# Latent attention with values stationary, probabilities divided before the transposes, ScalarE evicting the keys, and another order of its stage

## The reference

```python
def mla(h, pos, w_down, q_norm, kv_norm, w_uq, w_ukv, w_out):
    cq, ckv, kr = jnp.split(h @ w_down, [256, 512], axis=-1)
    q = (rms_norm(cq, q_norm) @ w_uq).reshape(bsz, seq, 16, 64 + 32)
    q_nope, q_rope = q[..., :64], rope(q[..., 64:], pos)
    kv = (rms_norm(ckv, kv_norm) @ w_ukv).reshape(bsz, seq, 16, 64 + 64)
    k_nope, v = kv[..., :64], kv[..., 64:]
    k_rope = rope(kr, pos)
    # in blocks of 128 queries
    s = (einsum('bqhd,bkhd->bhqk', qn_i, k_nope) + einsum('bqhr,bkr->bhqk', qr_i, k_rope)) * 96 ** -0.5
    p = jax.nn.softmax(s, axis=-1)
    o = einsum('bhqk,bkhd->bqhd', p, v)
    return o.reshape(bsz, seq, 16 * 64) @ w_out

x = layer_norm(ALPHA * x + (1 + gate) * mla(x * (1 + scale) + shift), g, b)
```

## Time and profile before

| What | Value |
|---|---|
| Median of 3 runs | 1023.76 us (1023.01 to 1024.12) |
| Profiled execution, whole | 1025.26 us |
| Its span in the profile | 1023.2 us |
| PE, DVE, ACT busy in the span | 98%, 79%, 49% |
| Scores of unit 0 to the transposes `next` | 749.7 us to 824.3 us |

### The profile page before, as it was taken

The page is one execution under the profiler, slowest core; times in us unless marked ns, Lnnn a source line. Parts: engine busy times, 40 slices in busy tenths (PEclk is TensorE's granted clock), DMA queues, the critical chain, the costliest instruction groups (busy, mean ns, idle before and its releaser), DMA issues.

```text
span 1023.2 us, 13210 instructions
## 1 busy us (share of the span) xinstructions
PE 998.2 (98%) x5024; PEld 830.2 (81%) x5024; DVE 806.8 (79%) x1203; ACT 502.9 (49%) x756; POOL 51.4 (5%) x101
## 2 busy tenths in 40 slices
PE   7899999999999999999999999999999999999996
PEld 5678888889978778888887888888888888888885
DVE  5889898689889887888779878877878886666455
ACT  3654345376767544343546343443677654443430
POOL 1000000013311000000000000000100000000000
PEclk9999999999999999999999999999999999999999
DMA  9999999558343699989848997974332559767431
GB/s 353 400 350 407 385 380 319 184 176 293 112 147 120 208 358 364 300 289 355 280 142 320 361 317 278 374 263 143 93 98 91 171 188 325 238 201 244 167 124 42
DMA packets 72545, 254.80 MB, mean 249 GB/s; under 512 B 8801, under 2 KB 10337, under 8 KB 72482
## 3 DMA queue, kind: packets, MB, share of 16 engines
q1 hardware_dynamic: 68946, 242.91, 66.5%
q0 software_dynamic: 3104, 10.39, 3.4%
q10 hardware_dynamic: 432, 0.66, 0.2%
HBM read 252.85 MB, written 1.07 MB: 248 GB/s over the span
## 4 chain that ended last, share of the span: by engine, by line
PE 88%; DMA 4%; DVE 4%; ACT 2%; issue 1%; SPq 0%; DVEq 0%; ACTq 0%
PE bank L1921 27%; PE bank L1925 26%; PE bank L1924 26%; DMA w_raw<-in_w_dram 3%; PE bank L2332 2%; DMA arena<-in_ada_w_dram 1%; PE bank L2043 1%; PE bank L2066 1%; PE bank L2033 1%; PE bank L2054 1%; PE bank L2154 1%; PE bank L2184 0%; ACT arena L929 0%; PE bank L1894 0%; DVE w_lo L1243 0%
## 5 line engine op out<-in xcount | busy, mean ns | idle before, releaser
L1243 DVE TENSOR_TENSOR w_lo<-w_raw,w_hi 128x2048 fp32r<-128x2048 f32 (+3 forms) x162 | 345.0, 2148 | 22.8 <-ACT w_hi L895 22.7
L1921 PE MATMUL bank<-w_hi,hT_hi 128*128 128x512 f32 (+3 forms) x880 | 350.8, 399 | 9.5 <-DVE hT_lo L1780 6.4
L1925 PE MATMUL bank<-w_lo,hT_hi 128*128 128x512 f32 (+3 forms) x880 | 338.7, 385 | 0.0
L1924 PE MATMUL bank<-w_hi,hT_lo 128*128 128x512 f32 (+3 forms) x880 | 338.2, 384 | 0.0
L895 ACT ACTIVATE w_hi<-w_raw 128x2048 fp32r<-128x2048 f32 (+3 forms) x152 | 281.1, 1852 | 37.5 <-DMA w_raw<-in_w_dram 27.5
L1921 PEld LDWEIGHTS bank<-w_hi,hT_hi 128*128 128x128 f32 x880 | 165.8, 188 | 45.0 <-DVE hT_lo L1780 8.0
L1925 PEld LDWEIGHTS bank<-w_lo,hT_hi 128*128 128x128 f32 x880 | 165.7, 188 | 33.4
L1924 PEld LDWEIGHTS bank<-w_hi,hT_lo 128*128 128x128 f32 x880 | 166.2, 189 | 28.6
L1017 ACT ACTIVATE arena<-bank 128x256 f32<-128x256 f32 x88 | 33.6, 382 | 277.7 <-PE bank L1925 277.6
L1262 DVE SCALAR_TENSOR_TENSOR arena<-arena,c_row 128x1024 f32<-128x1024 f32 x131 | 155.8, 1218 | 8.2 <-ACT c_row L970 7.2
L1921 PE MATMUL bank<-w_hi,fT_hi 128*128 128x512 f32 x352 | 138.3, 393 | 1.7 <-DVE fT_lo L1801 1.7
(11 more groups left out here) (243 smaller groups left out, 867.3 us busy)
## 6 DMA issues: line engine op xcount, KB each, us to landing
w_raw<-in_w_dram SPq DMA_DIRECT2D x306, 512.0 KB, 5.8
arena<-in_ada_w_dram SPq DMA_DIRECT2D x132, 512.0 KB, 7.5
m_o<-in_ada_w_dram SPq DMA_DIRECT2D x10, 512.0 KB, 7.1
gate_row<-gate_scratch POOLq DMA_DIRECT2D x6, 512.0 KB, 5.2
arena<-in_ln_g_dram POOLq DMA_DIRECT2D x6, 512.0 KB, 4.6
arena<-in_ln_b_dram POOLq DMA_DIRECT2D x6, 512.0 KB, 6.5
w_raw<-in_w_dram SPq DMA_DIRECT2D x8, 256.0 KB, 2.8
w_raw<-in_w_dram SPq DMA_DIRECT2D x8, 192.0 KB, 2.8
```

The costliest lines, as they stand in the source:

```text
L1243: op = nc.vector.tensor_tensor(w_lo[:, j0 % RING, c], raw_of(j0)[:, c], w_hi[:, j0 % RING, c].bitcast(F32), ALU.subtract)
L1921: mm = nc.tensor.matmul(dst, a_hi, b_hi, start=start, stop=False)
L1924: nc.tensor.matmul(dst, a_lo, b_hi, start=False, stop=False)
L1925: return nc.tensor.matmul(dst, a_hi, b_lo, start=False, stop=stop)
```

## The change

It touches the latent attention alone.

1. V: values are stationary and transposed probabilities move. The outputs of the two heads, 64 rows each, go to partitions 0 to 63 and 64 to 127 of bank 5, already transposed. `owin` and its 16 transposes are gone.
2. The division moves ahead: a new VectorE step D takes the reciprocal and multiplies `mP` (128x256 for each head) before P; P waits for it (`p_ready`) where it waited for the exponentials.
3. ScalarE copies the transposed probabilities to `mpT` and the transposed keys out of bank 7 (both VectorE's before); VectorE still evicts the queries.
4. ScalarE writes the high part of V's output into `hT_hi`, VectorE the low part in a step of its own (`values_lo`), and V of the next unit waits for that.
5. The exponential's table is loaded by a small instruction behind `uq` (0, 1).
6. The latents move to blocks 4 to 7 of `hT`, the first tile's output to banks 0 and 1.
7. The order is new: the projections start with step 10 where they started with step 12, and nearly all stand between units. The low parts of the weights move with them. The residual and the normalization of tile 0 (`end`) come before V of unit 15, and the second half of slot 16 and a scaling of x come behind it.

```diff
-            before = {1: (("rq", (1, 1)),), 3: (("qkT", (1, 0)),), 4: (("uq", (2, 0)), ("rq", (2, 0))),
-                      12: (("out", (0, 0, 0)),), 13: (("out", (0, 0, 1)),), 14: (("out", (1, 0, 0)),), 15: (("out", (1, 0, 1)),),
-                      16: (("out", (2, 0, 0)),)}
+            yield from (("S", 0), ("S", 1), ("ukv", (1, 1)), ("qkT", (1, 0)), ("P", 0), ("S", 2), ("P", 1), ("V", 0), ("S", 3),
+                        ("hi", (8, 0, 1)), ("qkT", (1, 1)), ("P", 2), ("V", 1))
+            before = {4: (("uq", (2, 0)),), 5: (("uq", (2, 1)),), 6: (("ukv", (2, 0)),),
+                      7: (("qkT", (2, 0)), ("ukv", (2, 1))), 8: (("uq", (3, 0)), ("uq", (3, 1))),
+                      9: (("ukv", (3, 0)), ("ukv", (3, 1))), 10: (("out", (0, 0, 0)), ("qkT", (3, 1)), ("out", (0, 0, 1))),
+                      11: (("out", (0, 1)),), 12: (("out", (1, 0)),), 13: (("out", (2, 0)),), 14: (("out", (1, 1)),),
+                      15: (("out", (3, 0)),), 16: (("out", (2, 1)),)}
-            yield from (("out", (3, 0)), ("split", (16, 0, 1)), ("owin", (1, 1)), ("end", 0), ("out", (0, 1)), ("out", (1, 1)),
-                        ("out", (2, 1)), ("next", 0), ("out", (3, 1)))
+            yield from (("next", 0), ("out", (3, 1)))
...
+            inner = {4: (("rq", (2, 0)),), 5: (("rq", (2, 1)),), 6: (("lo", (10, 0, 1)),), 8: (("rq", (3, 1)),),
+                     9: (("qkT", (3, 0)),), 10: (("qkT", (3, 1)),), 11: (("lo", (12, 1)),), 12: (("lo", (13, 0)),),
+                     13: (("lo", (14, 0)),), 14: (("lo", (15, 0)),)}
+            outer = {5: (("lo", (9, 0, 1)),), 6: (("qkT", (2, 0)),), 7: (("qkT", (2, 1)), ("rq", (3, 0))),
+                     8: (("lo", (11, 0)),), 9: (("lo", (11, 1)), ("scale", (0, 0))), 10: (("lo", (12, 0)), ("scale", (0, 1))),
+                     11: (("scale", (1, 0)),), 12: (("lo", (13, 1)),), 13: (("lo", (14, 1)),), 14: (("lo", (15, 1)),)}
+            for n in range(4, 16):
+                yield "S", n
                 yield from inner.get(n, ())
+                yield "D", n
+                yield "V", n - 2
                 yield from outer.get(n, ())
-            yield from (("split", (16, 0, 1)), ("owin", (1, 1)), ("end", 0))
+            yield from (("end", 0), ("V", 15), ("lo", (16, 1)), ("scale", (1, 1)))
...
+        M_UNITS = {(0, 0): 2, (0, 1): 4, (1, 0): 6, (1, 1): 8, (2, 0): 10, (3, 0): 12, (2, 1): 14, (3, 1): 16}
+        M_KEYS = {0: (2, 1), 2: (2, 2), 4: (4, 3), 6: (4, 4), 8: (6, 5), 10: (8, 7), 12: (8, 6), 14: (8, 8)}
...
+                        elif stage == "exp":
+                            nc.scalar.activation(early_silu[:, :], neg_half[:, :], ACT.Exp)
+                        elif stage == "qkT":
+                            nc.scalar.activation(mkT[g % 2][:, :, t * P:(t + 1) * P],
+                                                 banks[7][0:96, :].rearrange("p (h n) -> p h n", h=4), ACT.Copy)\
+                                .then_inc(mk_ready, 1)
+                        elif stage == "P":
+                            nc.scalar.activation(mpT[:, m % 2, :], banks[4][:, :], ACT.Copy).then_inc(pT_ready, 1)
                         elif stage == "V":
+                            nc.scalar.activation(hT_hi[:, k, tok], banks[5][:, 0:P], ACT.Copy).then_inc(o_hi, 1)
...
                     elif stage == "end":
                         residual(s)
-                        norm(s, 0)
+                        values_lo(14)
+                        norm(s, 0, lambda: split_lo(base[s] + 16, (0,)))
+                    elif stage == "D":
+                        b = m % 2
                         dve.wait_ge(s_exp, A0 + m + 1)
+                        step(nc.vector.reciprocal(rden[:, m % 4, :], den[:, m % 4, :]))
+                        step.wait()
+                        for a in range(2):
+                            op = nc.vector.tensor_scalar(mP[:, b, a, :], mP[:, b, a, :], rden[:, m % 4, a:a + 1], None, ALU.mult)
+                        op.then_inc(p_ready, 1)
+            def values_lo(m):
+                dve.wait_ge(o_hi, O0 + m + 1)
+                nc.vector.tensor_tensor(hT_lo[:, k, tok], banks[5][:, 0:P], hT_hi[:, k, tok].bitcast(F32),
+                                        ALU.subtract).then_inc(o_ready, 1)
...
                     elif stage == "P":
-                        pe.wait_ge(s_exp, A0 + m + 1)
+                        pe.wait_ge(p_ready, m + 1)
...
-                            pe.wait_ge(o_att, A0 + m)
-                        for a in range(2):
-                                mm = nc.tensor.matmul(banks[5][:, a * 64:a * 64 + 64], mpT[:, m % 2, c:c + P],
-                                                      v_nat[g][:, kt, h * 64:h * 64 + 64],
-                                                      start=kt == 0, stop=kt == 1)
+                            pe.wait_ge(o_ready, O0 + m)
+                        for kt in range(NT):
+                            for a in range(2):
+                                mm = nc.tensor.matmul(banks[5][a * 64:a * 64 + 64, 0:P], v_nat[g][:, kt, h * 64:h * 64 + 64],
+                                                      mpT[:, m % 2, c:c + P], start=kt == 0, stop=kt == 1,
+                                                      skip_group_check=True)
```

More of the change, by code:

```diff
@@ L273, in build @@
         qk4_tr = sem("qk4_tr")
-        qk4_ready = sem("qk4_ready")
+        mk_ready = sem("mk_ready")
+        mq_ready = sem("mq_ready")
         c_ready = sem("c_ready")
@@ L457, in mla_plan @@
                     yield stage, m
-                    if (n, stage) == (1, "E"):
-                        yield "ukv", (1, 1)
-                    if n == 9 and stage in ("S", "V"):
-                        yield "qkT", (3, int(stage == "V"))
+                    if (n, stage) == (9, "S"):
+                        yield "qkT", (3, 0)
                 yield from behind.get(n, ())
-            yield from (("out", (3, 0)), ("split", (16, 0, 1)), ("owin", (1, 1)), ("end", 0), ("out", (0, 1)), ("out", (1, 1)),
-                        ("out", (2, 1)), ("next", 0), ("out", (3, 1)))
+            yield from (("next", 0), ("out", (3, 1)))
         def mla_vector_plan():
@@ L558, in out_banks @@
         def out_banks(s, t):
-            return ([banks[0], banks[5]], [banks[6], banks[7]])[t] if subs[s][0] == "hyb" else Y[t]
+            if subs[s][0] == "ffn":
+                return Y[t]
+            return ([banks[0], banks[5 if subs[s][0] == "hyb" else 1]], [banks[6], banks[7]])[t]
         def entry_banks(s):
@@ L1404, in residual @@
                 dve.wait_ge(h_ready, 4 * (2 * s + 2))
+                area = scratch2 if subs[s][0] == "mla" else scratch
                 for half in range(2):
                     c = slice(half * 512, half * 512 + 512)
-                    step(nc.vector.tensor_tensor(scratch[:, c], out_banks(s, 0)[half][:, :], gate_row[:, c], ALU.mult))
+                    step(nc.vector.tensor_tensor(area[:, c], out_banks(s, 0)[half][:, :], gate_row[:, c], ALU.mult))
                 for half in range(2):
@@ L1699, in mla @@
                             k, tok = 2 * v + n, slice(t * P, (t + 1) * P)
-                            op = nc.vector.scalar_tensor_tensor(out=hT_lo[:, k, tok], in0=c_bank(t, v)[:, n * P:(n + 1) * P],
-                                                                scalar=norm_col[:, k:k + 1], in1=hT_hi[:, k, tok].bitcast(F32),
+                            at = M_LATENT + k
+                            op = nc.vector.scalar_tensor_tensor(out=hT_lo[:, at, tok], in0=c_bank(t, v)[:, n * P:(n + 1) * P],
+                                                                scalar=norm_col[:, k:k + 1], in1=hT_hi[:, at, tok].bitcast(F32),
                                                                 op0=ALU.mult, op1=ALU.subtract)
@@ L2010, in mla @@
                             w, tok = slice(k * width, (k + 1) * width), slice(t * P, (t + 1) * P)
-                            mm = product(bank[:, 0:width], hT_hi[:, 2 * v + k, tok], hT_lo[:, 2 * v + k, tok],
+                            at = M_LATENT + 2 * v + k
+                            mm = product(bank[:, 0:width], hT_hi[:, at, tok], hT_lo[:, at, tok],
                                          w_hi[:, j0 % RING, w], w_lo[:, j0 % RING, w], k == 0, k == 1)
@@ L2069, in mla @@
-                        mm.then_inc(pv_done, 1)
-                    elif stage == "owin":
-                        t, half = m
-                        pe.wait_ge(o_att, A0 + (8 if half == 0 else 12 + 4 * t))
-                        if half == 0:
-                            pe.wait_ge(qk4_ready, 16)
-                        else:
-                            pe.wait_ge(o_ready, O0 + t + 1)
-                        for k in range(4):
-                            c = (4 * half + k) * P
-                            mm = nc.tensor.transpose(banks[6 + t][:, k * P:(k + 1) * P], m_o[:, t, c:c + P], ident[:, :])
-                        mm.then_inc(o_tr, 1)
```

(1 more changed line is left out.)

93 lines of the change are left out of this document (37 added, 56 removed), and 13 rows, old and new, of tables (MLA_SCALE, behind, outer).

## The result

| | before | after |
|---|---|---|
| Median | 1023.94 us (1023.01 to 1024.41, 4 runs) | 1038.89 us (1035.03 to 1040.34, 4 runs) |
| Ratio after to before | | 1.014, 95% interval 1.0126 to 1.0153 |
| Profiled execution, whole; its span | 1025.26; 1023.2 us | 1040.34; 1038.3 us |

The change costs 15.0 us in the median, 15.1 between the profiled executions. The forecast was 1035.0, its range 1028 to 1040.

The account below looks back on a forecast made before the run. TensorE, busy 98% of the span, was taken as the bound. Waits of 16.1 us plus 0.1 for a format change, less 4.9 gained, gave +11.3: 1023.8 to 1035.1 in the median, eight in ten within 1028 to 1040.

Parts of the forecast that it names:

- out(0,0,0): Projection product behind qkT (3,0): waits 2.2 us for slot 11, whose second half VectorE does behind the unit's chain.
- out(1,0): Projection product: waits 0.9 us for the second half of slot 12, which stands behind the maximum on VectorE.
- out(2,0): Projection product: waits 3.1 us for slot 13's second half, behind D and unit 10's low part on VectorE.
- out(2,1): Projection product near the end: waits 2.0 us for the low part of unit 13's output.
- next: Next sublayer's start after the attention: waits 2.9 us for normalized x, behind statistics, a moved half slot 16 and scaling.
- V, with the changes of form: V in each unit: halves of the array overlap, so 0.78 us, 1.0 us gained over 16 units.
- second entry of the FFN: Behind next: TensorE waits 1.3 us for the second tile's normalization on VectorE.
- rival 2: The clock falls behind two long new waits: nine slow products, 1.8 us an event, +15, 1039; chance 0.11.
- The chain of a unit: Other engines' work from S's start: exponentials done at 2.7 us, D 3.5, V's low part 3.95, half slot 5.1.
- D ends at 3.5: Division on VectorE behind the exponentials: 0.8 us, between 0.6 and 1.0, ending 3.5 us after S starts.
- Rival 1: Halves don't run side by side in V: 1.05 us, 0.27 more a unit; about +14.5, 1038.5; chance 0.10.
- Faster: Rival: VectorE keeps ahead of the weights, so waits for slots 11 to 13 and tail vanish; 1020.5; chance 0.07.

Follow-up runs that it names:

- e7: e2 with 10 needless matmuls of 512 columns before out(0,0,0) as well; 1034.76 us.
- e2: The changed kernel with needless 512-column matmuls on TensorE in its waits before out(2,0), out(2,1), V of unit 15 and next; 1035.96 us.
- e1: The changed kernel with low parts of slots 11 to 13 earlier on VectorE and high parts of slots 13 and 14 whole on ScalarE; 1028.68 us.
- e8: The changed kernel without the division: no reciprocal, no multiplication of the probabilities, P waits for the exponentials; 1037.61 us.
- e12: The changed kernel with both heads' outputs of V in partitions 0 to 63, using the same half of the array's columns; 1042.39 us.
- e9: The changed kernel's steps in a new order: weight splits, key evictions, projections, residual, normalization and tail moved; 1020.25 us, ratio 0.9968 to before.

## Why the prediction held, and where it was off

Its sum was 11.3 us for the waits and gains alone, and the forecast left the clock to a rival. Both came: 11.0 us are what e7 shows without the clock, and 4 more the clock's. The mechanism was right; that the sum comes within 0.3 of e7 is in part luck, since three smaller errors offset each other: the late starts of after add up to 15.6 us where it has 14.8 (without the FFN's entry), the steps gain 0.7 more at V, and the entry costs 0.5 less. Step by step, idle times as the rows of after have them:

| Step | predicted | after |
|---|---|---|
| out(0,0,0) | 2.2 | 2.61 |
| out(0,1) | 0.3 | 0.40 |
| out(1,0) | 0.9 | 0.98 |
| out(2,0) | 3.1 | 3.08 |
| out(2,1) | 2.0 | 1.86 |
| V of unit 15 | 1.0 | 0.79 |
| `next` | 2.9 | 3.27 |
| qkT (0,1), P of units 0 to 2, qkT (2,0) | 0.3, 0.4, 0.1 | 0.15, 0.56, 0 late |
| S of unit 4, P of unit 4 | 1.1, 0.5 | 0.76 and 0.33 idle; 0.9 and 0.5 late |
| V, with the changes of form | 0.78 | 0.59 + 0.09 + 0.03; 0.59 + 0.09 + 0.10 where S follows |
| second entry of the FFN | 1.3 | 0 (0.8 in e2 and e7) |
| half-rate clock | rival 2: 3.6 | 6.1 lost in the profile, 4.1 net in the median (e7) |

- **The chain of a unit** was right, as e1 shows by taking its consequence away. From S of unit 12 (802.83): maximum at 1.07, the division's end at 3.7, the low part of V's output at 3.6 to 3.85 (they overlap; predicted 3.5 and 3.95), half slot 13 to 5.0 (5.1). For unit 9 that low part starts at 3.97, since ScalarE evicts the keys of qkT (3,0) in between; this makes 2.61 of 2.2.
- **D's place in the chain.** The prediction let its bounds (0.2 either way in five waits) carry 1 us of the range. e8 shows that it hardly counts: ScalarE's two copies are as long. The step "D ends at 3.5" was right, but of no effect beside V's copy at 3.6.
- **V** was taken from rows on halves of rows and proved right for halves of columns. It is entered 0.09 late (P to V 0.53 for the 0.44 of the earlier trace rows), and an S right behind it takes 0.97 for 0.87 (755.74 to 756.71). But mostly a product stands there, and it loses only 0.03, so that V costs 0.71 for 0.81 to 0.84: 1.7 us gained over the 16 units, where the prediction has 1.0. The Trainium skill (TensorEngine Tiling (Array Packing), Key Properties) says that changing the mode drains the engine. The trace has a price at each change that fits it: 0.09 ahead, about 0.15 inside the 0.59 (four pairs at 0.109 are 0.44), and 0.03 to 0.10 behind, 0.3 us a unit in all. Rival 1 would have been e12, and its price, 14.5 over before where the forecast was 11.3, agrees with what e12 adds.
- **`next`** waited 0.4 longer than summed. The prediction let half slot 16 hide GpSimd's part of the normalization, taken as 0.67 us. But beside that half slot GpSimd's one small instruction takes 1.47 us where it took 0.56 with VectorE idle, and VectorE waits another 0.45 for it. First before, then after:

```profile
822.31 0.56 POOL L789 TENSOR_TENSOR rstd<-var_eps,neg_half 128x1 f32<-128x1 f32 x1 [82.04 <-DVE var_eps L1465]
```

```profile
835.23 1.47 POOL L799 TENSOR_TENSOR rstd<-var_eps,neg_half 128x1 f32<-128x1 f32 x1 [96.02 <-DVE var_eps L1475]
...
836.73 0.81 DVE L1491 TENSOR_SCALAR x<-x,mean_var,rstd 128x1024 f32<-128x1024 f32 x1 [0.45 <-POOL rstd L799]
```

- **The clock** is the term that was missing in the sum. Rival 2 had it at two places with nine products each, 0.2 us a product. The 0.2 is right (0.43 for 0.23); there are three places, and the first, with 12 products and the scores behind, costs 2.8, not 1.8. It was put beside the forecast, as an alternative, where it comes on top of it. The Trainium skill (TensorE: Matmul & The Clock Gate, HAM oscillation) warns of it for idle gaps between bursts. The trace and e7 agree that idle time does it, but here single gaps of 1.86 us were enough at times, shorter than the gaps that the section names.
- **The FFN's entry** (1.3) doesn't show in after. VectorE does reach it 2.33 behind `next` (2.4 predicted), but TensorE's out(3,1) is slow then and covers it. With the clock up (e2, e7) it is 0.8. Such terms don't simply add: here a slow stretch hid the wait behind it.
- ***Faster*** named the point that decides: half slot 13 ending by 2.1 behind S of unit 12. It ended at 5.0. e1 makes that condition true, e9 the whole rival, 1020.25 for its 1020.5.

## What to carry to other kernels

When a step moves to other engines, sum its chain from the start of the unit and set against it what TensorE has between two units: here 3.6 to 4 us of chain want 2.9 us of products besides the 2.1 of the unit. An instruction for later work (a weight split) belongs ahead of the chain or in a gap before it, never behind the chain's last step if its reader comes next, and never ahead of its own input in a strict queue: one slot ahead of its input cost 4 us, and moving five half slots took two thirds of the loss away. Count that idle TensorE can cost twice: once as the wait, and, behind some waits of 1.9 us and more, once more as products at half rate.
